# Depthwise convolution of the odd mixer: 24 taps of its fourth channel tile as diagonal matmuls on TensorE, GpSimd's part gone, two attention heads stacked in the partitions

## The reference, cut to what matters

```python
def odd_mixer(x, w_in, forget_b, dw_w, dw_b, cn_g, cn_b, w_out):
    p = x @ w_in                                   # 1024 -> 2568 columns
    q, k, v = (p[..., i * D_C:(i + 1) * D_C].reshape(bsz, s, H_C, HEAD_DIM) for i in range(3))  # 8 heads of 64
    log_f = jax.nn.log_sigmoid(p[..., 3 * D_C:3 * D_C + H_C] + forget_b)
    y_c = forgetting_attention(q, k, v, log_f).reshape(bsz, s, D_C)   # causal softmax attention
    y_d = conformer_conv(p[..., 3 * D_C + H_C:], dw_w, dw_b, cn_g, cn_b)
    return jnp.concatenate([y_c, y_d], axis=-1) @ w_out

def conformer_conv(p_d, dw_w, dw_b, cn_g, cn_b):
    h = p_d[..., :D_D] * jax.nn.sigmoid(p_d[..., D_D:])   # 512 channels
    h = causal_dwconv(h, dw_w) + dw_b                     # 31 taps, each channel by itself
    return jax.nn.silu(layer_norm(h, cn_g, cn_b))
```

## Time and profile before

| what | value |
|---|---|
| runs | 1337.38, 1341.44, 1343.13 us; median 1341.44 |
| the profiled execution | 1341.74 us, its span 1339.9 us |
| mean granted clock of TensorE | 0.971 |
| busy | TensorE 94%, VectorE 61%, ScalarE 45%, GpSimd 14% |

### The profile page before, as it was taken

The page is one execution under the profiler, slowest core; times in us unless marked ns, Lnnn a source line. Parts: engine busy times, 40 slices in busy tenths (PEclk is TensorE's granted clock), DMA queues, the critical chain, the costliest instruction groups (busy, mean ns, idle before and its releaser), DMA issues.

```text
span 1339.9 us, 22211 instructions
## 1 busy us (share of the span) xinstructions
PE 1254.6 (94%) x9112; PEld 1151.7 (86%) x9112; DVE 822.1 (61%) x1214; ACT 597.5 (45%) x891; POOL 189.0 (14%) x147
## 2 busy tenths in 40 slices
PE   5799999999999998999989989999989788999996
PEld 1577777778888897999989989999989778999996
DVE  2788934446788866554456775554467996555544
ACT  3332433337566434452245354344354555444433
POOL 1233400000000000001100311110004961111100
PEclk9799999999999998999999999999989898999999
DMA  9557211113322254552253435555524303455550
GB/s 389 230 228 270 107 64 63 64 63 104 117 95 95 95 189 152 179 184 95 68 184 127 171 111 191 180 175 182 190 101 148 126 32 126 161 185 188 188 188 34
DMA packets 27472, 195.55 MB, mean 146 GB/s; under 512 B 3192, under 2 KB 3328, under 8 KB 3968
## 3 DMA queue, kind: packets, MB, share of 16 engines
q1 hardware_dynamic: 26496, 191.90, 39.9%
q10 hardware_dynamic: 896, 2.50, 0.5%
HBM read 193.33 MB, written 1.05 MB: 145 GB/s over the span
## 4 chain that ended last, share of the span: by engine, by line
PE 82%; DVE 10%; ACT 3%; issue 1%; DVEq 0%; POOL 0%; ACTq 0%
PE ps L413 24%; PE ps L415 23%; PE ps L414 23%; PE ps L455 4%; DVE acc L1942 3%; PE ps L651 2%; DVE w_lo L1421 1%; PE ps L551 1%; DVE xconv L1527 1%; PE ps L639 1%; DVE rstd L1751 1%; ACT w_hi L892 1%; PE ps L470 1%; DVE xconv L1536 1%; DVE xconv L1500 0%
## 5 line engine op out<-in xcount | busy, mean ns | idle before, releaser
L892 ACT ACTIVATE w_hi<-ring 128x1024 fp32r<-128x1024 f32 x312 | 326.3, 1057 | 469.6 <-PE ps L415 391.1
L1421 DVE TENSOR_TENSOR w_lo<-ring,w_hi 128x1024 fp32r<-128x1024 f32 x288 | 351.8, 1235 | 294.6 <-ACT w_hi L892 289.5
L413 PE MATMUL ps<-x_hi,w_hi 128*128 128x256 f32 x1216 | 350.3, 288 | 20.2 <-DVE x_lo L1760 20.2
L414 PE MATMUL ps<-x_lo,w_hi 128*128 128x256 f32 x1216 | 349.2, 287 | 0.0
L415 PE MATMUL ps<-x_hi,w_lo 128*128 128x256 f32 x1216 | 348.9, 287 | 0.0
L413 PEld LDWEIGHTS ps<-x_hi,w_hi 128*128 128x128 f32 x1216 | 238.5, 196 | 22.5 <-issue 22.5
L414 PEld LDWEIGHTS ps<-x_lo,w_hi 128*128 128x128 f32 x1216 | 238.4, 196 | 0.0
L415 PEld LDWEIGHTS ps<-x_hi,w_lo 128*128 128x128 f32 x1216 | 238.3, 196 | 0.0
L413 PE MATMUL ps<-g_hi,w_hi 128*128 128x256 f32 x608 | 171.3, 282 | 2.5 <-POOL g_lo L1365 1.0
L415 PE MATMUL ps<-g_hi,w_lo 128*128 128x256 f32 x608 | 170.5, 280 | 0.0
L414 PE MATMUL ps<-g_lo,w_hi 128*128 128x256 f32 x608 | 169.7, 279 | 0.0
(11 more groups left out here) (290 smaller groups left out, 1927.2 us busy)
## 6 DMA issues: line engine op xcount, KB each, us to landing
ring<-in_weights SPq DMA_DIRECT2D x156, 1024.0 KB, 4.9
o_sb<-in_weights SPq DMA_DIRECT2D x10, 1024.0 KB, 6.7
ada_room<-in_weights SPq DMA_DIRECT2D x10, 1024.0 KB, 7.3
V<-in_weights SPq DMA_DIRECT2D x3, 1024.0 KB, 22.4
dft<-in_dft ACTq DMA_DIRECT2D x1, 1026.0 KB, 5.5
X<-in_x SPq DMA_DIRECT2D x1, 1024.0 KB, 5.0
ctx_room<-in_ctx SPq DMA_DIRECT2D x1, 1024.0 KB, 7.5
xconv<-in_weights SPq DMA_DIRECT2D x1, 1024.0 KB, 27.7
```

What stands on the lines that cost most here:

```text
L413: mm(dst, w_h, x_h, start=start, stop=False, skip_group_check=True)
L414: mm(dst, w_h, x_l, start=False, stop=False, skip_group_check=True)
L892: do(w_hi[:, q % 2, part], ring[:, q % RING, part], ACT.Copy).then_inc(S("hi_ready"), 1)
L1421: v.tensor_tensor(w_lo[:, q % 2, part], ring[:, q % RING, part], w_hi[:, q % 2, part], ALU.subtract).then_inc(S("lo_ready"), 1)
```

## The change

GpSimd no longer takes part. ScalarE builds 24 diagonal matrices (128 x 128, the identity scaled by a tap's weights) in the space that `logit` uses later. TensorE multiplies them with the shifted rows of tile 3 behind slot `odin` 4, ScalarE moves the sum with the bias into `acc31`, and VectorE does taps 24 to 30 of tile 3 as before, now among the others. The two heads of a pair are written to the two halves of the partitions, so that `round_attention` and `split_attention` are one instruction each. The mean's column sum moves behind slot `odout` 1, and `lo` of slots `odout` 2 and 3 moves to VectorE. ScalarE's and VectorE's lists are reordered to suit.

```diff
-POOL_TAPS = 24
+PE_TAPS = 24
@@ tensor engine
+                elif hd == 3:
+                    pe.wait_ge(S("taps_moved"), 1)
...
-                at = SEQ * b
-                mm(ps[:, c % 2, at:at + SEQ], vtok[:, 0, c * P:(c + 1) * P], probT[:, b, 0, :],
+                part, own = slice(FD * b, FD * (b + 1)), slice(FD * hd, FD * (hd + 1))
+                mm(ps[part, c % 2, 0:SEQ], vtok[:, 0, own], probT[:, b, 0, :],
...
                 slot(STARTS["odin"], odd_in, t, t)
+                if t == 4:
+                    pe.wait_ge(S("diagonals"), 1)
+                    pe.wait_ge(S("odin_moved"), KH)
+                    for k in range(PE_TAPS):
+                        last = mm(ps[:, 7, 0:SEQ], diag[:, k, :], pad_a[:, KH - 1, k + 2:k + 2 + SEQ],
+                                  start=(k == 0), stop=(k == PE_TAPS - 1))
+                    last.then_inc(S("taps_summed"), 1)
...
-                        pe.wait_ge(S("probT_moved"), 7)
-                        column_sum(conv_mean, ones_h[:, :], lambda k: acc31[:, k, :], KH, S("norm_in"),
-                                   S("norm_mean"), since("in", "conv"))
...
             for hd in range(6, FH):
                 attend(hd)
+            mixed_slot(1)
+            column_sum(conv_mean, ones_h[:, :], lambda k: acc31[:, k, :], KH, S("norm_in"),
+                       S("norm_mean"), since("in", "conv"))
             column_sum(conv_var, ones_h[:, :], lambda k: sq[:, k, :], KH, S("norm_squares"),
                        S("norm_var"), since("squares", "conv"))
-            mixed_slot(1)
             mixed_slot(2)
@@ scalar engine
             feed_forward(0)
+            for k in range(PE_TAPS):
+                last = do(diag[:, k, :], ident, ACT.Copy, scale=vcol("dw_w", k * KH + KH - 1))
+            last.then_inc(S("diagonals"), 1)
...
                 if t == 5:
+                    act.wait_ge(S("taps_summed"), 1)
+                    do(acc31[:, KH - 1, :], ps[:, 7, 0:SEQ], ACT.Identity, bias=vcol("dw_b", KH - 1))\
+                        .then_inc(S("taps_moved"), 1)
                     act.wait_ge(S("cum_ready"), 1)
...
+            weighed(3)
             hi(STARTS["odout"])
             move_odin(8)
-            exponentials(4)
-            weighed(3)
-            exponentials(5)
             for hd in range(2):
                 move_turned(hd)
-            exponentials(6)
+            for hd in range(4, 7):
+                exponentials(hd)
...
             round_attention(2)
+            round_attention(3)
+            hi(STARTS["odout"] + 2)
             for k in range(KH):
                 act.wait_ge(S("norm_centred"), since("centred", "conv") + k + 1)
                 do(sq[:, k, :], acc31[:, k, :], ACT.Square).then_inc(S("norm_squares"), 1)
-            hi(STARTS["odout"] + 2)
-            round_attention(3)
+            hi(STARTS["odout"] + 3)
             act.wait_ge(S("norm_var"), since("var", "conv") + 1)
...
-            hi(STARTS["odout"] + 3)
@@ gpsimd: chain of lines 1387 to 1405 removed (24 taps, lo of slots odout 2 and 3)
@@ vector engine, convolved(k0, k1)
+                    if k == 20:
+                        dve.wait_ge(S("taps_moved"), 1)
+                    if 20 <= k < TAPS - 5:
+                        taps(k + 4, (3,))
@@ vector engine, the order (excerpt)
-            convolved(28, TAPS - 1)
-            dve.wait_ge(S("pool_order"), 2 * POOL_TAPS - 1)
...
+            split_attention(1)
+            lo(STARTS["odout"] + 1)
+            convolved(25, 27)
+            for c in range(2, KH):
+                split_attention(c)
+            convolved(27, TAPS - 1)
+            final_tap(0)
...
+            final_tap(3)
+            lo(STARTS["odout"] + 2)
             dve.wait_ge(S("norm_mean"), since("mean", "conv") + 1)
             for k in range(KH):
                 v.tensor_tensor(acc31[:, k, :], acc31[:, k, :], conv_mean, ALU.subtract)\
                     .then_inc(S("norm_centred"), 1)
-            for c in range(2, KH):
-                split_attention(c)
+            lo(STARTS["odout"] + 3)
             dve.wait_ge(S("norm_root"), since("root", "conv") + 1)
```

More of the change, by code:

```diff
@@ L281, in program @@
         acc31 = sc("acc31", (P, KH, SEQ))
+        diag_stack = ExitStack()
+        diag = tensors(diag_stack)("diag", (P, PE_TAPS, P))
+        diag_stack.close()
         logit = sc("logit", (P, FH, 2, SEQ))
@@ L814, in attend @@
                         pe.wait_ge(S("attn_split"), c - 1)
-                at = SEQ * b
-                mm(ps[:, c % 2, at:at + SEQ], vtok[:, 0, c * P:(c + 1) * P], probT[:, b, 0, :],
+                part, own = slice(FD * b, FD * (b + 1)), slice(FD * hd, FD * (hd + 1))
+                mm(ps[part, c % 2, 0:SEQ], vtok[:, 0, own], probT[:, b, 0, :],
                    start=True, stop=False, skip_group_check=True)
-                mm(ps[:, c % 2, at + P:at + SEQ], vtok[:, 1, c * P:(c + 1) * P], probT[:, b, 1, P:SEQ],
+                mm(ps[part, c % 2, P:SEQ], vtok[:, 1, own], probT[:, b, 1, P:SEQ],
                    start=False, stop=True, skip_group_check=True).then_inc(S("attn_done"), 1)
@@ L1265, in round_attention @@
                 act.wait_ge(S("attn_done"), 2 * c + 2)
-                chain.step(do(g_hi[0:FD, KH + c, :], ps[0:FD, c % 2, 0:SEQ], ACT.Copy))
-                do(g_hi[FD:P, KH + c, :], ps[FD:P, c % 2, SEQ:2 * SEQ], ACT.Copy).then_inc(S("attn_rounded"), 1)
+                do(g_hi[:, KH + c, :], ps[:, c % 2, 0:SEQ], ACT.Copy).then_inc(S("attn_rounded"), 1)
             for t in range(8):
@@ L1387, in _ @@
             feed_forward(0)
[L1389 to L1404, removed]
             feed_forward(1)
@@ L1964, in split_attention @@
                 dve.wait_ge(S("attn_rounded"), c + 1)
[L1965 to L1971, removed]
+                v.tensor_tensor(g_lo[:, KH + c, :], ps[:, c % 2, 0:SEQ], g_hi[:, KH + c, :], ALU.subtract)\
+                    .then_inc(S("attn_split"), 1)
             def maximum(hd):
@@ L2002, in _ @@
                 .then_inc(S("forget_moved"), 1)
-            convolved(5, 8)
+            convolved(5, 7)
             lo(STARTS["odin"] + 6)
-            convolved(8, 10)
             dve.wait_ge(S("forget_log"), 1)
@@ L2014, in _ @@
                 .then_inc(S("cum_ready"), 1)
-            convolved(10, 11)
+            convolved(7, 10)
             lo(STARTS["odin"] + 7)
-            convolved(11, 14)
+            convolved(10, 13)
             lo(STARTS["odin"] + 8)
-            convolved(14, 16)
+            convolved(13, 15)
             for hd in range(3):
@@ L2024, in _ @@
                 sum_inverse(hd)
-            convolved(16, 18)
+            convolved(15, 17)
             maximum(3)
-            convolved(18, 19)
-            lo(STARTS["odout"])
-            convolved(19, 20)
+            convolved(17, 18)
             maximum(4)
@@ L2033, in _ @@
             maximum(6)
-            convolved(20, 21)
+            lo(STARTS["odout"])
             sum_inverse(4)
             sum_inverse(5)
-            convolved(21, 22)
+            convolved(18, 19)
             sum_inverse(6)
-            convolved(22, 24)
+            convolved(19, 22)
             split_attention(0)
+            convolved(22, 23)
+            maximum(7)
+            convolved(23, 24)
+            sum_inverse(7)
             convolved(24, 25)
[L2042 to L2045, removed]
             split_attention(1)
-            convolved(28, TAPS - 1)
-            dve.wait_ge(S("pool_order"), 2 * POOL_TAPS - 1)
-            late = range(POOL_TAPS, TAPS - 1)
-            for k in late:
-                if k > late[2]:
-                    chain.join()
-                taps(k, (3,))
-                if k in late[:2]:
-                    taps(TAPS - 3 + k - POOL_TAPS, (2,))
-                if k - POOL_TAPS in (2, 3, 4):
-                    final_tap(k - POOL_TAPS - 2)
-            chain.join()
+            lo(STARTS["odout"] + 1)
[4 more added lines that the diff above has]
+            final_tap(0)
+            chain.join()
+            taps(TAPS - 3, (2,))
+            final_tap(1)
+            chain.join()
+            taps(TAPS - 2, (2,))
+            chain.join()
+            final_tap(2)
             final_tap(3)
-            lo(STARTS["odout"] + 1)
+            lo(STARTS["odout"] + 2)
             dve.wait_ge(S("norm_mean"), since("mean", "conv") + 1)
@@ L2081, in _ @@
                         .then_inc(S("conv_split"), 1)
-            dve.wait_ge(S("lo_ready"), 2 * STARTS["ffi1"])
             lo(STARTS["ffi1"])
```

## The result

| | before | changed |
|---|---|---|
| runs | 6, 1337.38 to 1343.13 us | 5, 1346.82 to 1352.32 us, and one of 3190.57 |
| median | 1341.71 us | 1350.96 us of all six, 1349.71 of the five |
| ratio of the runs | | 1.0067, 95% interval 1.0045 to 1.0089 |
| the profiled execution, its span | 1341.74, 1339.9 us | 1352.32, 1350.5 us |

The changed kernel is 9.0 us slower by the ratio, and the interval makes it 6 to 12; by the medians it is 9.3, or 8.0 with the five runs.

The account below looks back on a forecast made before the run. VectorE was taken to set the pace behind slot odin 3, TensorE ahead of it. +7.8 (step 1) +2.4 (last tap and tail) +2.3 (clock) = +12.5 us on 1341.74 gave 1354.2, predicted as 1354, range 1345 to 1360.

Parts of the forecast that it names:

- step 1: Odd mixer's start: ScalarE's diagonals at 0.30 us each (bounds 0.15, 0.41) stall TensorE 5.3, plus 2.5 low clock: +7.8 us.
- the last tap and tail: Mixer's end: last tap at 1097.6 against 1094.9, slot odout 2 at 1109.6, 2.4 us later than before.
- the low clock of the last two slots: From slot odout 2: TensorE, idle from 1102.3 to 1109.6, then pays another 2.3 us at low clock.
- Step 2: Behind slot odin 4: 24 taps take TensorE 10.6 us, spending VectorE's freed 11 and TensorE's freed 8; odout 0 at 1081.6.
- the signs: Marks expected in the profile after, among them VectorE's waits for w_hi grown from some 3 us to about 8.
- TensorE's freed 8 us: Ahead of slot odout 0: 8 us of TensorE idle freed, spent with VectorE's 11 on 10.6 us of taps.
- Step 3: From 1080.7 to the mixer's end: later last tap and tail +2.4 us, low clock +2.3, together +4.7.
- VectorE's relief: Rival: freed of GpSimd's disturbance, VectorE ends its taps some 8 us earlier; -6 us, 1336; chance 8%.
- Cheap diagonals: Rival at the mixer's start: diagonals at 0.15 us each give +6.4, 1348, or 1346 with no delay; chance 15%.
- The low clock in more places: Rival: taps or slot odout 0 run at 1.2 GHz behind gaps, diagonals at 0.41; 1359 to 1361 us; chance 15%.
- Taps at half the price: Rival on TensorE's taps: 5.3 us less on the path, so +7, 1349; chance 7%.
- The port's rule: GpSimd and two-SBUF-input VectorE instructions lock a shared port pair; GpSimd's leaving frees VectorE of some 11 us.

Follow-up runs that it names:

- e7_heads: The kernel before with only the two heads of a pair put in the halves of the partitions; 1338.22 us, ratio 0.9984.
- e10: e8_fill_all without the taps moved ahead: tail in the order of the kernel before, taps in the changed kernel's order; 1337.95 us, ratio 0.9987.
- e1_early: The changed kernel with the 24 diagonals built in threes during ffo0, no longer ahead of the odd mixer; 1345.35 us, ratio 1.0026.
- e8_fill_all: e1_early with 22 VectorE taps moved ahead into its waits and the tail in the order of the kernel before; 1329.72 us, ratio 0.9923.
- e2_nopool: The kernel before with 23 of GpSimd's 24 taps left out and nothing in their place; 1333.55 us, ratio 0.9957.
- e3_nopetaps: The changed kernel with 23 of the 24 diagonal matmuls left out, diagonals still built; 1344.30 us, ratio 1.0027.
- e5_spread: e1_early with the 24 diagonal matmuls in four groups of six behind slots odin 4 to 7; 1343.48 us, ratio 1.0019.
- e11: e8_fill_all with the 24 diagonals built ahead of the odd mixer, as in the changed kernel; 1337.43 us, ratio 0.9978.
- e4_tail: The changed kernel with lo of slots odout 2 and 3 and hi(odout+3) moved out of the tail's chain; 1348.39 us, ratio 1.0063.

## Why the prediction was right, and where its sizes were off

**The whole.** +12.5 us were predicted for the profiled execution, and the mixer shows +10.3; the ratio of the runs says +9.0. The three steps came as forecast, in place and order. The 2.2 us too many lie in step 1 (7.8 put, 6.7 measured), in the last tap and tail (2.4 put, 1.9 measured) and in the low clock of the last two slots (2.3 put, 1.65 measured). The experiments add up to nearly the same: GpSimd's going -7.6, the matmuls +7.5, the diagonals +6.8, the two heads -0.7 (e7_heads), the tail's order +4.8 (e10 against e1_early), together +10.8 against 10.3. That the parts add is assumed, and e8_fill_all shows that two of them need not.

**Step 1, the diagonals.** The stream came at 0.30 us each (24 in 7.12), in the middle between the bounds, and the gap was 5.16 us against 5.3. What was off is the price of the clock behind it: 2.5 us put, but slot 2 took 7.26 us (1010.74 to 1018.00) instead of 5.7, so 1.6. The step cost 6.7 us by the marks ((1018.00 - 991.58) less (1010.96 - 991.26)), 6.8 and 7.0 by the two experiments, 7.8 by my sum.

**Step 2, the taps on TensorE.** 10.2 us (1033.17 to 1043.35) against 10.6. Taking off the shift of 7.0 us (6.7, and 0.3 for the mixer's later start), slot `odout` 0 began at 1081.3 (predicted 1081.6). That relief and price come out even is borne out by e2_nopool (7.6) and e3_nopetaps (7.5). VectorE's own work from 1029.9 (1022.8 before) to the last tap is 59.0 us (59.5 put). Its waits there are 15.6 us, 11.7 of them for `w_hi` (before: 3.3 in all), against 14.8 for the waits that steps 2 and 3 name together with the 3.3 of before; the "about 8" for `w_hi` among the signs was too low. At `lo(odin+7)` it waited 4.96 and 1.59 us, against 4.2 and 1.8. What I had not seen is how hard TensorE's bound holds: I had put TensorE's freed 8 us beside the matmuls as if those were slack, and e5_spread showed that there is none.

**Step 3, the tail.** With the same shift off, the last tap ended at 1097.5 (1097.6 predicted), the reciprocal began at 1104.8 (1105.0) and slot `odout` 2 at 1109.1 (1109.6); before it was 1107.23. The two slots behind it took 1.65 us more than before for the clock, against 2.3 put.

**The rivals.** VectorE's relief does not reach the end, since waits for `w_hi` took it up. VectorE's rows, 1018 to 1110, of before and then of the changed kernel:

```profile
DVE w_lo L1421 <- ACT w_hi L892: 7.2, 4, 2.3
```

```profile
DVE w_lo L1420 <- ACT w_hi L903: 18.6, 9, 5.0
```

Cheap diagonals: no, 0.30 each. The low clock in more places: the granted clock is 1.00 from 1020 to 1100. Taps at half the price: no, two records each and 0.42 us for each tap. The port's rule that I cited from the Trainium skill (SBUF — State Buffer, "SBUF: two separate sides") fits as far as VectorE's taps go, at 571 ns on average beside GpSimd's and 474 without; that the cause is a lock on the ports is not shown by any run here. The relief was real at the end too, 7.6 us in e2_nopool, and the diagonal matmuls took it up.

**What I missed** is the better half: that the change could pay. It took three things together: the diagonals in ffo0 (7.0 us by e11), some 20 taps further ahead in VectorE's list, and the tail in the order of the kernel before. I had read VectorE's new waits as a cost, not as room. One rival stands untested: the kernel before with its own taps moved ahead. It too had waits for `w_hi` and 15.1 us of idle time on TensorE, so how much of the 9.0 us of e8_fill_all is owed to the change, and how much to the new order, is open.

## What to carry to other kernels

Work that is moved to another engine has a preparation too: look at what stands behind the preparation in its engine's list at the time it runs (24 copies cost 7 us at the head of the mixer and nothing that could be seen three at a time in the stage before). When a bound engine is relieved, look at its list again: waits that appear in it are the place for its movable work. Look at what follows in the same step, since here the taps moved ahead brought 3.4 us alone, the tail's order 4.8, and both 12.5. Count a stage from mark to mark in the profile when executions differ by more than the effect.

## What the runs showed of the hardware that was not expected

- The stretch at the level of 1.2 GHz behind a gap does not go by the gap's length: 5.1 us behind 4.10 us of standing still (from 991.58), 2.9 us behind 5.16 (from 1010.74), 3.3 us behind 6.54, and 5.9 us behind 5.43 in e4_tail. The four cost 1.6 to 2.7 us each against the same slots at full clock. A shorter wait was followed by the low level too: in the kernel before TensorE waited 1.92 us ahead of 1039.73, and its granted clock was 0.50 from 1041 to 1044, while it was busy.
- An f32 matmul of 64 weight columns, written to half of the partitions, is not cheaper here than one of 128, and the next starts later: an attend's two matmuls and the step to the turn behind them took 0.80 us (0.49 + 0.31) in the changed kernel against 0.65 us (0.43 + 0.22) before. The mean duration by form, of before and of the changed kernel, 1077 to 1100:

```profile
L816 PE MATMUL ps<-probT,vtok 128*128 128x256 f32 x12 | 3.6, 381 | 0.0
```

```profile
L821 PE MATMUL ps<-probT,vtok 128*64 128x256 f32 x16 | 4.5, 404 | 0.0
```
